# Where the tiles of a long matmul kernel lie in SBUF, moved by lines of 64 bytes

## The reference, cut to what matters

```
gates  = sigmoid(g_logits.reshape(B, S, 4, D) + b_merge)
merged = gates[:, :, 0] * (y_a @ w_br_pool) + gates[:, :, 1] * (y_b @ w_br_swa) \
       + gates[:, :, 2] * (y_c @ w_br_gla)  + gates[:, :, 3] * (y_m @ w_br_mem)
x      = x + rms_norm_2(merged @ w_out, g_post)
```

## Time and profile before

| | |
|---|---|
| runs | 3202.24 us median of 2 (3202.04 and 3202.45) |
| span of the profiled execution | 3201.1 us |
| TensorE busy | 3186.8 us, 100% (rounded) of the span |
| ScalarE, VectorE, GpSimd busy | 1290.4, 1341.0, 1063.6 us |
| read from HBM | 333.49 MB, 113 GB/s over the span |
| chain that ended last | TensorE 97%, of it L785 59% of the span |

### The profile page before, as it was taken

One profiled execution on the slowest core, in us unless ns is written; L12 is line 12 of the kernel. 1 busy time (PEld: TensorE's weight loads), 2 busy tenths in 40 slices (PEclk: granted clock), 3 DMA queues, 4 the chain that ended last, 5 costly groups with the idle time before them and its releaser, 6 DMA issues.

```text
span 3201.1 us, 41942 instructions
## 1 busy us (share of the span) xinstructions
PE 3186.8 (100%) x15426; PEld 2665.0 (83%) x15426; DVE 1341.0 (42%) x1885; ACT 1290.4 (40%) x1992; POOL 1063.6 (33%) x460
## 2 busy tenths in 40 slices
PE   9999999999999999999999999999999999999999
PEld 8877888888888888888888888888888888888887
DVE  3573321113123534401111111144369999999802
ACT  6543322333235534332323324422335555555532
POOL 7633333333443434443433433344430000000043
PEclk9999999999999999999999999999999999999999
DMA  8622323233433423243333333433444444444442
GB/s 291 179 79 67 86 66 86 79 85 98 120 107 100 144 74 93 80 134 102 86 86 92 87 84 92 133 104 92 150 133 134 140 137 138 134 134 134 143 153 99
DMA packets 546540, 364.49 MB, mean 114 GB/s; under 512 B 18809, under 2 KB 505209, under 8 KB 545145
## 3 DMA queue, kind: packets, MB, share of 16 engines
q1 hardware_dynamic: 522912, 321.50, 35.3%
q10 hardware_dynamic: 23512, 41.40, 3.7%
HBM read 333.49 MB, written 29.36 MB: 113 GB/s over the span
## 4 chain that ended last, share of the span: by engine, by line
PE 97%; DVE 1%; ACT 1%; POOL 0%; issue 0%; DMA 0%; DVEq 0%; ACTq 0%; POOLq 0%
PE proj L785 59%; PE s L1556 10%; PE t L1556 8%; PE s L1600 3%; PE proj L1556 1%; PE s L1255 1%; PE proj L1600 1%; PE t L1600 1%; PE t L810 1%; PE s L854 1%; PE s L847 1%; PE t L1255 1%; PE proj L1255 1%; PE s L1080 1%; PE s L1061 1%; PE s L948 1%
## 5 line engine op out<-in xcount | busy, mean ns | idle before, releaser
L756 POOL TENSOR_TENSOR w_lo<-raw,w_hi 128x1024 fp32r<-128x1024 f32 x431 | 1061.5, 2477 | 2111.6 <-ACT w_hi L1637 2084.7
L785 PE MATMUL proj<-ht_hi,w_hi 128*128 128x512 f32 x2400 | 956.0, 398 | 0.0
L785 PE MATMUL proj<-ht_hi,w_lo 128*128 128x512 f32 x2400 | 935.6, 390 | 0.0
L785 PE MATMUL proj<-ht_lo,w_hi 128*128 128x512 f32 x2400 | 934.8, 389 | 0.0
L1637 ACT ACTIVATE w_hi<-raw 128x1024 fp32r<-128x1024 f32 x396 | 404.3, 1053 | 386.3 <-PE proj L785 223.9
L785 PEld LDWEIGHTS proj<-ht_lo,w_hi 128*128 128x128 f32 x2400 | 451.2, 188 | 95.1 <-issue 4.8
L785 PEld LDWEIGHTS proj<-ht_hi,w_lo 128*128 128x128 f32 x2400 | 450.6, 188 | 95.8
L785 PEld LDWEIGHTS proj<-ht_hi,w_hi 128*128 128x128 f32 x2400 | 451.0, 188 | 94.7 <-issue 4.8
L3593 DVE TENSOR_TENSOR w_lo<-raw,w_hi 128x1024 fp32r<-128x1024 f32 x128 | 156.1, 1219 | 16.0 <-ACT w_hi L2507 14.9
L2511 ACT ACTIVATE w_hi<-t_w 128x1024 fp32r<-128x1024 f32 x96 | 101.9, 1061 | 106.1 <-DVE t_w L3611 53.3
L3593 DVE TENSOR_TENSOR w_lo<-t_w,w_hi 128x1024 fp32r<-128x1024 f32 x96 | 116.9, 1217 | 12.8 <-ACT w_hi L2511 12.8
(11 more groups left out here) (693 smaller groups left out, 4948.7 us busy)
## 6 DMA issues: line engine op xcount, KB each, us to landing
raw<-in_w_in_dram SPq DMA_DIRECT2D x404, 512.0 KB, 3.8
raw<-in_w_out_dram SPq DMA_DIRECT2D x64, 512.0 KB, 3.9
g_zt<-z_spill SPq DMA_DIRECT2D x64, 256.0 KB, 3.9
raw<-in_xa_wkv_dram SPq DMA_DIRECT2D x16, 512.0 KB, 7.2
raw<-in_w_mem_kv_dram SPq DMA_DIRECT2D x16, 512.0 KB, 3.8
raw<-in_w_br_gla_dram SPq DMA_DIRECT2D x16, 512.0 KB, 4.0
z_spill<-z_early ACTq DMA_DIRECT2D x32, 256.0 KB, 3.1
raw<-in_w_br_pool_dram SPq DMA_DIRECT2D x16, 512.0 KB, 4.2
```

The lines of the kernel that those rows point to most:

```text
L756: pool.tensor_tensor(w_lo[:, slot, :], raw[:, slot, :], w_hi[:, slot, :].bitcast(F32), ALU.subtract).then_inc(lo_done, 1)
L785: ins = pe.matmul(dst, w, x[:, kt, c0:c1], start=first and n == 0 and m == 0, stop=last and n == len(kts) - 1 and m == 2)
```

## The change

Four small tiles move forward in the order of the places: small goes between the weights and ht, and par, count16 and gate_bias between ht and the stage region. All else keeps its order. The total is the same up to rounding, and no instruction, loop, wait or DMA is changed except for the addresses in them.

```diff
         w_hi = keep("w_hi", [P, RING, HALF], F32R)
         w_lo = keep("w_lo", [P, RING, HALF], F32R)
-
+        small = keep("small", [P, 48])
         ht_hi_at, ht_lo_at = take(KT * T * 4), take(KT * T * 4)
         ht_hi = at("ht_hi", [P, KT, T], ht_hi_at, F32R)
         ht_lo = at("ht_lo", [P, KT, T], ht_lo_at, F32R)
+        par = keep("par", [P, NPARAM])
+        count16 = keep("count16", [P, 16])
+        gate_bias = keep("gate_bias", [4, 2])
         m_at = take(M_REGION)
         m_end = m_at + M_REGION
         raw = keep("raw", [P, RING, HALF])
...
         k2, v2 = at("k2", [P, 4, M], kv2_at), at("v2", [P, 4, 2, P], kv2_at + 4096)
-
         dist = keep("dist", [P, T])
         ident_at = place[0]
         ident = keep("ident", [P, P])
         ones = keep("ones", [P, P])
-        par = keep("par", [P, NPARAM])
-        small = keep("small", [P, 48])
-        count16 = keep("count16", [P, 16])
-        gate_bias = keep("gate_bias", [4, 2])
         assert place[0] <= nc.sbuf_usable_end
```

## The result

The changed kernel takes 3250.48 us (median of 2 runs, 3250.24 to 3250.73) against 3202.24 us: slower by 48 us, ratio 1.015, 95% interval 1.0133 to 1.0167. The direction was as forecast, and so was the cause in the main: the places of the two operands set the matmul's rate. The size was not: +23 us were expected, and 48 came, and the rule for the places was taken with the wrong period.

The account below looks back on a forecast made before the run. TensorE bounds the kernel (97% of the chain), so time is a sum of matmul start-to-start intervals; 18 + 5.5 + 2 - 3.4 + 0.8 = +23 us on 3201.1 us, forecast 3225 us, range 3125 to 3275.

Parts of the forecast that it names:

- sign of being wrong: The prediction is wrong if projections lie outside 227.5 to 231 ns, or time moves without the chain's intervals moving.
- That placement sets the rate: Operands' places change matmul intervals: yp's 385 matmuls at 233.3 ns against 226.7 with the same shape and code line.
- Rival 3: yp's slower rate comes from something else, placement does not matter: 3202 us, within 5; chance 0.2.
- That the relation counts, not the line: What counts is the gap: line of the weights being loaded less the moving operand's line, modulo 8 (64-byte lines).
- The price of ht at gap 5: Projections and gate products, ht moving, gap 0 to 5: 228.9 ns, +2.2 ns on 8224 matmuls, +18 us.
- Rival 1: The heavy side: new gaps settle at the yp rate, 233.3 ns, about +72 us, 3274 us; chance 0.17.
- yh, yl, s1 and s2: Branch and gate products with these moving, gap 0 to 2: 231 ns, +4.3 ns on 1280 matmuls, +5.5 us.
- w moving: ht as weights (L1600, L1255, L847), gap 0 to 3: 228 ns, +1.3 ns on 1344 matmuls, +2 us.
- yp and s4: These moving, gap 1 to 3: from 233.3 to 228 ns on 640 matmuls, -3.4 us.
- 256 columns: Gate products and kv rows of 256 columns, some 2200 matmuls: 0, with -9 to +9 us.
- Plain float32, the other engines, the DMAs: Attention and recurrence matmuls, VectorE, GpSimd, ScalarE and DMAs: no effect or hidden by TensorE, priced at 0.
- Rival 2: Streams three lines apart run free at 216 ns: 127 us faster, 3075 us (half: about 3121); chance 0.2.

## Why the prediction was right in the cause and wrong in the size

The changed kernel took 3250.48 us against a forecast of 3225, inside the range from 3125 to 3275. That it stayed inside is owed to the width of the range and not to the sum. The sign of being wrong that the prediction named was met: the projections lie at 233.3 ns, outside 227.5 to 231.

- **That placement sets the rate.** Right, and shown: with the same code, clock and shapes, a piece of 792 projections takes 179.56 us with ht on line 4, 181.31 on line 1 and 184.81 on line 3. Rival 3 (nothing changes) falls. The Trainium skill, in "TensorE: Matmul & The Clock Gate", section "Step-by-step: what each phase is for", says that loading the next weights doesn't take from the running matmul. The traces don't bear that out for fp32r: with the moving operand left on one line, weights moved by one to three lines change the interval by 2 to 7 ns of 227. How much of the 226.7 ns at gap 0 is owed to the load is not shown.
- **That the relation counts, not the line.** Right: all tiles shifted together by three lines, 3201.63 us.
- **The price of ht at gap 5, taken as 228.9 ns, +18 us.** This is the step that failed. It measured 233.3 ns and +45.4 us. The two rows I took it from were not rows of that state. The four intervals at gap 5 on mlg_w come in the midst of a walk in which the gap changes every second matmul. After a change a stream needs several intervals to settle (five behind a group of 256 columns), so such a row tells of the change, not of the place. And I counted lines modulo 8, because a weight slice is 512 bytes, and took the 228.9 ns of gap 7. With a period of four, gap 7 is gap 3, and gap 5 is gap 1, whose steady rate stood in the earlier trace rows with 385 matmuls: 233.3 ns. Nothing in the trace of before said eight. Rival 1, at 0.17, was right on ht's steady rate. Its price was too high: 54.8 us for ht where 45.4 came, 9 for ht as weights where 2.5 came, and +72 us in all for 48.
- **yh, yl, s1 and s2, +5.5 us.** +6.4. The rate I took, 231 ns, was 232.4 in the steady piece.
- **w moving, +2 us.** +2.5, at 229.0 ns for 228.
- **yp and s4, -3.4 us.** -2.6, at 228.9 ns for 228.
- **o, +0.8 us.** +0.5, at the 233.3 ns that was forecast.
- **256 columns, 0 with 9 either way.** -4.1 us, inside the bounds: other places are cheaper there, as the 4 ns in the earlier trace rows hinted.
- **Plain float32, the other engines, the DMAs, 0.** Right, -1.0 us for all other matmuls. GpSimd's 2477 ns, which should have stood, became 2511, at no cost.
- **Rival 2, the overlap is freed (3075 us).** Wrong in the kernel and in the matmuls alone: of 16 steps of 16 bytes none comes below 226.7 ns. Of the places tried for 512 columns, none is below gap 0.

With the measured +45.4 us for ht in place of +18, and -4.1 for the 256 columns, the sum of +23 becomes +46 us. That ht's 8224 matmuls paid 5.5 ns on average and not the 6.6 of the steady pieces comes from the 1460 that were not at 226.7 ns before either, and that paid next to nothing.

## What to carry to other kernels

In a stream of fp32r matmuls with 128 weight columns and 512 moving ones, put the moving tiles and the weight tiles at the same place modulo 256 bytes: here this was worth 6.6 ns of 233 for each steady matmul, and 1.3% of the kernel between ht on line 4 and ht on line 3. A tile length that isn't a multiple of 256 bytes (44480 here) or a small tile between two large ones changes it for all that lie behind. For 256 and 384 moving columns another gap was cheaper, so measure the shape at hand, in pieces of tens of matmuls in a steady stream, and never from a few intervals after a change.

## What the runs showed that I had not expected

- The period of 256 bytes, half of a weight slice: gaps 0 and 4 at 227 ns, 1 and 5 at 233 ns.
- The matmul stream has a memory. At a gap of 3 modulo 4 it runs at 228.9 ns in one stretch and at 233.3 ns in another of the same kernel. In the gate products of the kernel before, after a group of 256 columns, the eight matmuls of 512 that follow need five intervals of 228 to 236 ns before they come to 227. What decides between the two steady rates was not tried.
- Fewer weight columns don't help: 32 columns gave 231.7 ns at gap 0, where 128 gave 226.7. So that the excess is the load's traffic is not shown. What is shown is that the interval depends on the two operands' places in fp32r, and that in bf16 and plain float32 it does not. Which part of the memory or of the engine the two share stays open.
- GpSimd's subtraction went from 2477 to 2511 ns with the change and to 2525 ns with the region, raw and xy moved and ht left. It was hidden, and why it is so was not tried.
